# Two blocks on one core: the seventh bunch of experts kept out of four buffers, one weight layout for all bunches, and the normed x written spread

## The reference, cut to what matters

```python
x = layer_norm(DEEPNORM_ALPHA * x + y, ln1_g[layer], ln1_b[layer])
y = hierarchical_moe(x, ...)            # two experts of 32 a token
...
def block_ffn(args):                    # weights 1024x256, 1024x256, 256x1024 each
    xb, e = args
    return (jax.nn.silu(xb @ w_gate[e]) * (xb @ w_up[e])) @ w_down[e]
```

## Time and profile before

| what | value |
|---|---|
| median of three runs | 734.92 us |
| the profiled execution | 740.1 us |
| its span | 738.2 us |
| TensorE (PE) busy | 660.7 us, 89% |
| VectorE (DVE) busy | 352.3 us, 48% |
| ScalarE (ACT) busy | 330.4 us, 45% |
| moved by DMA | 167.84 MB, mean 227 GB/s |

### The profile page before, as it was taken

One profiled execution on the slowest core, in us unless ns is written; L12 is line 12 of the kernel. 1 busy time (PEld: TensorE's weight loads), 2 busy tenths in 40 slices (PEclk: granted clock), 3 DMA queues, 4 the chain that ended last, 5 costly groups with the idle time before them and its releaser, 6 DMA issues.

```text
span 738.2 us, 11783 instructions
## 1 busy us (share of the span) xinstructions
PE 660.7 (89%) x4605; PEld 512.8 (69%) x4606; DVE 352.3 (48%) x817; ACT 330.4 (45%) x776; POOL 43.8 (6%) x57
## 2 busy tenths in 40 slices
PE   6989999999899999969856999998979999889986
PEld 5867998689545644616421589877859899778876
DVE  1543657646511021101000357887774577886643
ACT  3465655531111121202010253777865556888642
POOL 6001000000000000000000132010000020100000
PEclk9999999999999999989885999999989999999999
DMA  9995325896999999999769938026263080081301
GB/s 273 340 287 184 124 65 173 270 304 249 378 387 417 408 415 412 412 417 408 308 209 417 342 103 291 9 72 214 82 204 115 1 265 22 11 275 58 115 1 58
DMA packets 94681, 167.84 MB, mean 227 GB/s; under 512 B 4270, under 2 KB 75712, under 8 KB 90528
## 3 DMA queue, kind: packets, MB, share of 16 engines
q1 hardware_dynamic: 92272, 160.88, 61.1%
q0 software_dynamic: 2224, 6.10, 2.5%
q10 hardware_dynamic: 128, 0.08, 0.0%
HBM read 165.96 MB, written 1.07 MB: 226 GB/s over the span
## 4 chain that ended last, share of the span: by engine, by line
PE 60%; SPq 12%; DVE 9%; DMA 8%; ACT 8%; issue 3%; DVEq 0%; ACTq 0%
PE psum L922 10%; SPq L786 10%; PE psum L923 10%; PE psum L924 10%; PE psum L1337 5%; PE psum L1293 4%; PE psum L1352 2%; PE psum L1227 2%; DMA values<-in_w_expert_up_dram 2%; DMA mixT<-in_w_expert_up_dram 2%; PE psum L965 2%; PE psum L1057 2%; DMA ring<-in_w_in_dram 2%; PE psum L1274 2%; DVE w_low L2349 2%
## 5 line engine op out<-in xcount | busy, mean ns | idle before, releaser
L922 PE MATMUL psum<-a_high,w_high 128*128 128x256 f32 x512 | 150.8, 295 | 9.1 <-DVE w_low L2349 4.6
L923 PE MATMUL psum<-x_low,w_high 128*128 128x256 f32 x512 | 146.0, 285 | 0.0
L924 PE MATMUL psum<-a_high,w_low 128*128 128x256 f32 x512 | 145.9, 285 | 0.0
L922 PEld LDWEIGHTS psum<-a_high,w_high 128*128 128x128 f32 x512 | 99.2, 194 | 18.9 <-issue 6.8
L2349 DVE TENSOR_TENSOR w_low<-ring,w_high 128x1024 fp32r<-128x1024 f32 (+1 forms) x73 | 100.9, 1394 | 17.9 <-ACT w_high L1677 17.9
L1677 ACT ACTIVATE w_high<-ring 128x1024 fp32r<-128x1024 f32 (+1 forms) x79 | 96.1, 1220 | 13.6 <-DMA ring<-in_w_in_dram 10.3
L923 PEld LDWEIGHTS psum<-x_low,w_high 128*128 128x128 f32 x512 | 99.4, 194 | 0.1
L924 PEld LDWEIGHTS psum<-a_high,w_low 128*128 128x128 f32 x512 | 99.3, 194 | 0.0
L1337 PE MATMUL psum<-ring,q_c 128*32 128x512 f32 x336 | 64.9, 708 | 27.0 <-DMA ring<-in_w_expert_up_dram 18.3
L922 PE MATMUL psum<-w_high,a_high 128*128 128x256 f32 x240 | 69.4, 289 | 0.7 <-DVE mix_low L2360 0.7
L1337 PEld LDWEIGHTS psum<-ring,q_c 128*32 128x32 f32 x336 | 16.6, 127 | 64.6 <-issue 63.9
(11 more groups left out here) (346 smaller groups left out, 1175.6 us busy)
## 6 DMA issues: line engine op xcount, KB each, us to landing
ring<-in_w_in_dram SPq DMA_DIRECT2D x36, 1024.0 KB, 9.0
ring<-in_w_expert_down_dram SPq DMA_DIRECT2D x22, 1024.0 KB, 17.3
ring<-in_w_expert_gate_dram SPq DMA_DIRECT2D x42, 512.0 KB, 12.6
ring<-in_w_expert_up_dram SPq DMA_DIRECT2D x42, 512.0 KB, 14.3
ring<-in_w_out_dram SPq DMA_DIRECT2D x12, 1024.0 KB, 5.1
ring<-in_w_mem_kv_dram SPq DMA_DIRECT2D x4, 1024.0 KB, 15.0
k_c<-in_w_expert_down_dram SPq DMA_DIRECT2D x3, 1024.0 KB, 17.4
xT<-in_w_expert_gate_dram SPq DMA_DIRECT2D x4, 512.0 KB, 11.0
```

Source lines behind the costliest of these rows:

```text
L922: pe.matmul(dst, left[0], right[0], start=first, stop=False)
L923: pe.matmul(dst, left[0], right[1], start=False, stop=False)
L924: return pe.matmul(dst, left[1], right[0], start=False, stop=last)
```

## The change

Four things change. `expert_slots` keeps bunch 6 (the seventh) out of the buffers 0 to 3; bunch 7 still takes them for its first four pieces. The gate and up weights of all bunches come in the layout of eight rows a partition. The first norm's centred values go to a part of `tiles` (`centred2`) instead of staying in `x_nat`, and `scaled_half` writes the normed x to `x_nat` spread: channel 8q + k to place 128k + q (`spread` is the view written, `folded_in` the ones read). For tt = 0 two such halves take the place of one whole row. All gathers then read 128 contiguous elements, and the diagonal products of bunch 0 read x through `spread`, so that the sum comes out in natural order. The second norm writes x in natural order as before.

```diff
--- before.py
+++ after.py
@@ -138,7 +138,6 @@
 MORE_SLOTS = (9, 10, 11)
 EXPERT_RING = len(FIRST_LOADS)
 PER_BUNCH = 12
-IN_ORDER = 2
 
 
 def expert_slots():
@@ -146,10 +145,16 @@
     at = [k for _, k in sorted(FIRST_LOADS)]
     free = [k for k in at if k not in ONCE]
     for i in range(len(at), PER_BUNCH * BUNCHES):
-        last = i >= PER_BUNCH * (BUNCHES - 1)
-        j = i % PER_BUNCH
-        at.append(next(k for k in free if not last or (k == NEXT_LAYERS[j] if j < AT_ONCE
-                                                       else k not in NEXT_LAYERS + MORE_SLOTS)))
+        b, j = divmod(i, PER_BUNCH)
+        if b < BUNCHES - 2:
+            k = free[0]
+        elif b == BUNCHES - 2:
+            k = next(k for k in free if k not in NEXT_LAYERS)
+        elif j < AT_ONCE:
+            k = NEXT_LAYERS[j]
+        else:
+            k = next(k for k in free if k not in NEXT_LAYERS + MORE_SLOTS)
+        at.append(k)
         free.remove(at[-1])
         free.append(at[-1])
     return at
@@ -473,6 +478,14 @@
         def bank(n):
             return psum[:, n, :]
 
+        def spread(row, half):
+
+            return row.rearrange("p (k q) -> p q k", k=KC)[:, P // 2 * half:P // 2 * half + P // 2, :]
+
+        def folded_in(row, half):
+
+            return row[:, 512 * half:512 * half + 512].rearrange("p (q k) -> p q k", k=KC)
+
         def c_(name):
             a, b = CONST[name]
             return const[:, a:b]
@@ -481,6 +494,7 @@
         slots = ring[:, :].rearrange("p (s k n) -> p s k n", s=RING, k=KC)
         x2 = x_nat[:, :].rearrange("p (t d) -> p t d", t=2)
         x4 = x_nat[:, :].rearrange("p (t k q) -> p t k q", t=2, k=KC)
+        centred2 = tiles[:, 0:2048].rearrange("p (t d) -> p t d", t=2)
         xT3 = xT[:, :].rearrange("p (k t) -> p k t", k=KC)
         x1T = q_c[:, :].rearrange("p (k t) -> p k t", k=KC)
         y_nat = tiles[:, 0:2048].rearrange("p (t d) -> p t d", t=2)
@@ -782,7 +796,7 @@
                 if j < GATE_UP:
                     half = j // AT_ONCE
                     for m, name in enumerate(("w_expert_gate", "w_expert_up")):
-                        w = ins[name][0, e].rearrange("(k p) n -> p k n" if b < IN_ORDER else "(p k) n -> p k n", p=P)
+                        w = ins[name][0, e].rearrange("(p k) n -> p k n", p=P)
                         sp.dma_start(to[:, SLOT // 2 * m:SLOT // 2 * m + SLOT // 2].rearrange("p (k n) -> p k n", n=DE),
                                      w[:, 4 * half:4 * half + 4, :]).then_inc(loaded[slot_of(n)], 16)
                 else:
@@ -1289,8 +1303,7 @@
                 for c in range(4):
                     k = 4 * half + c
                     for tt in range(2):
-                        x = x4[:, tt] if b < IN_ORDER else x2[:, tt, :].rearrange("p (q k) -> p k q", k=KC)
-                        mm = pe.matmul(dst[:, P * c:P * c + P], x[:, k, :], places2[:, tt, :],
+                        mm = pe.matmul(dst[:, P * c:P * c + P], x4[:, tt, k, :], places2[:, tt, :],
                                        start=(tt == 0), stop=(tt == 1))
                 mm.then_inc(gathered_ready, 1)
 
@@ -1424,7 +1437,7 @@
                     if b == 0:
                         for m in range(4):
                             pe.matmul(bank(m), diagonal[:, P * (m // 2):P * (m // 2) + P],
-                                      x2[:, m // 2, 512 * (m % 2):512 * (m % 2) + 512],
+                                      spread(x2[:, m // 2, :], m % 2),
                                       start=True, stop=False, skip_group_check=True)
                     if b + 1 < BUNCHES:
                         if b > MEM_AT:
@@ -2120,7 +2133,8 @@
                 dve.wait_ge(ready, 32)
                 dve.wait_ge(ln_var, 2 * n + tt + 1)
                 for half in range(2):
-                    op = dve.scalar_tensor_tensor(x_half(tt, half), values(tt, half), mv3[:, tt, 0:1],
+                    to = x_half(tt, half) if n else centred2[:, tt, 512 * half:512 * half + 512]
+                    op = dve.scalar_tensor_tensor(to, values(tt, half), mv3[:, tt, 0:1],
                                                   ln_row[:, 0, 512 * half:512 * half + 512], ALU.subtract, ALU.mult)
                 link(op)
 
@@ -2133,9 +2147,9 @@
 
             def scaled_half(tt, half):
 
-                xs = x_half(tt, half)
-                return dve.scalar_tensor_tensor(xs, xs, ln_rs[:, tt:tt + 1],
-                                                ln_row[:, 1, 512 * half:512 * half + 512], ALU.mult, ALU.add)
+                return dve.scalar_tensor_tensor(spread(x2[:, tt, :], half), folded_in(centred2[:, tt, :], half),
+                                                ln_rs[:, tt:tt + 1], folded_in(ln_row[:, 1, :], half),
+                                                ALU.mult, ALU.add)
 
             def logit_shift(tt):
 
@@ -2468,8 +2482,10 @@
                         tt = job[1]
                         dve.wait_ge(p_ready, j + 1)
                         centred(0, tt, ln1_in, x_half)
+                        dve.wait_ge(ln_rstd, tt + 1)
                         if tt == 0:
-                            scaled(0, 0)
+                            scaled_half(0, 0)
+                            scaled_half(0, 1).then_inc(ln_done, 1)
                         logit_shift(tt)
                         if tt == 1:
                             scaled_half(1, 0)
```

## The result

The changed kernel takes 729.62 us (median of 6 runs) against 736.37 us for the kernel before in 6 runs beside it: a ratio of 0.9899, 95% interval 0.9851 to 0.9946, which is 7.4 us less (the medians are 6.8 apart). One of its six runs took 904.85 us; it lies outside everything else and is not in the ratio. Two more series of the same changed kernel gave 0.9875 and 0.9905. So the kernel became faster, by about half of what was forecast (13.9 us), and 729.62 lies above the range of 716 to 728.5. The profiled execution has a span of 731.0 us, against 738.2 before.

What follows compares the result with a forecast made beforehand. The prediction took the expert stage as bound by transfers, with one self-made stop. Its terms, -13.9 + 1.0 - 1.0 = -13.9 us, led from the median of 734.92 to 721.0 us, range 716 to 728.5.

Steps and rivals of the forecast that it cites:

- What bounds the kernel: Expert stage: bound by transfers at about 413 GB/s, whose stream stops just once, behind bunch 6, for the kernel's own reasons.
- Part 1: Buffers of bunches 6 and 7: the hole in transfers goes, bunch 7's sigmoid at 393.24 instead of 407.18, -13.94 us.
- What is late next: the down weights ... so they aren't: Bunch 7's down weights, all landed at 394.6, would be in time for down products starting at 398.0.
- Part 2: Contiguous x in the gathers of bunches 2 to 7: 4.3 us less each, worth nothing because transfers hide it.
- Part 3: Spread writes of normed x and stepped diagonal products before and in bunch 0: 0 to 3.6 us, taken as +1.0.
- second term: Bunch 0's diagonal products reading x stepped: +4.3 us at 2.2 times, 3.7 covered by transfers, leaving 0 to 0.6.
- rival B: Spread access costs its upper bound: 723.6 us, or 724.6 without the 4 KB runs' microsecond; chance 0.10.
- A: Contiguous gathers slow the transfers by contention, 1.1 us each, six of them 6.6: 727.6 us; chance 0.14.
- C: The stream stops anyway, through SP's flag reading or another wait: some 731 us, at most no change; chance 0.06.
- Part 4: 4 KB runs in bunches 0 and 1 speed their gate and up pieces: -2.1 to 0 us, taken as -1.0.
- D: More idle time keeps the granted clock at its lower level through bunches 4 to 7: 749.5 us; chance 0.04.

Runs made afterwards that it cites:

- the buffers alone: The kernel before with the new choice of buffers and nothing else: ratio 0.9851, median 727.07 us; its repeat 0.9850, median 724.85 us.
- The held loads: The changed kernel with the first five loads of the second block held until bunch 7's down products begin to finish: ratio 0.9846.
- the first repeat: The changed kernel run once more with nothing altered: ratio 0.9875 to the kernel before, median 729.74 us against 738.02.
- The late diagonal products: The changed kernel with bunch 0's diagonal products behind its down products instead of ahead of its gather: ratio 0.9842, median 728.70 us.

## Why the prediction was half right

**What bounds the kernel** was right: transfers, with one stop of the kernel's own making. In the changed kernel TensorE is busy for 43.57 of 60 us between 300 and 360, where it was 48.55, and the stage's period did not move.

**Part 1, the hole, was right in size.** Forecast -13.94 us; the buffers alone gave bunch 7's sigmoid at 393.10 (forecast 393.24) and 13.5 and 12.2 us at the products behind the experts, 11.0 and 12.5 in the timed medians (727.07 against 738.02, 724.85 against 737.34). Some of that closeness is luck: I had TensorE start bunch 7's first half at 376.6, and it started at 384.37, 4.9 us after its last products of bunch 6. I read this as its own flag reading and branching, the only thing that the program has there; two packets of the instruction queues (379.97 and 381.79 in the changed kernel) fall into the same 4.9 us. I had counted this for SP alone. In return the second half, running right behind the first, took 3.64 us and not 6.34: the 2.7 us that I had left to the low end of the range came. In the buffers alone the weights for the second half landed at 387.64 and it began at 389.40, so there it was TensorE, and not the transfer of the forecast, that set the sigmoid's start.

**"What is late next: the down weights ... so they aren't" failed.** This is the first failed step. I put their landing at 394.6, the moment by which the stream's bytes would have moved, with nothing for the lag of a landing behind it. The held loads show how many bytes that is, since their queue is empty behind them: 127.6 MB from the span's start. The buffers alone have moved as much at 395.8 and land at 398.27, a lag of 2.4 us (2.8 in the repeat); the changed kernel at 399.5, 397.2 and 399.2, and it lands at 403.14, 400.98 and 402.36, lags of 3.7, 3.8 and 3.2. I had 3.4 us between landing and use. With the stream nearly on time it almost fits (waits of 0.53 and 1.20 us). In the changed kernel the stream is 2.6 to 4.9 us behind the forecast, and it is a wait of 3.1 us in all three profiles and, in two of them, a lower clock behind it (4.98 and 5.37 us instead of 3.67). The experiment with the held loads shows that at most 0.7 us of it is owed to the loads behind.

**Part 2** was right: the gathers of bunches 2 to 7 take 3.8 us instead of 7.8, and the period from bunch 5 to 6 is 30.46 us where it was 30.57, so they gain nothing.

**Part 3 was mis-sized in its second term, the diagonal products.** This is the second failed step. The spread writes were nearer the low end, as I had chosen: 1.11 against 0.75 us, and the way from the second row's residual to the start of gather 0 grew from 11.30 to 11.82 us, 0.5 us. For the diagonal products I had +4.3 us, covered by 1.5 MB of transfers still under way, so 0 to 0.6. They cost +3.45 us (7.08 against 3.63), and together with the 0.5 us of the writes the restart came 4.0 us later in the first repeat (218.18 against 214.21; 2.0 more in the first profile, which started later as a whole). The cover was even longer than I had read it: the last of the eight pieces landed 7.4 us behind the restart in the kernel before, since the queue still held others ahead of them, and 2.8 us behind it in the changed one. So the queue did not run empty, and by my reckoning next to nothing should have been lost. What failed is that reckoning, that a late issue costs only what the engines stand idle: after the restart they are busy, the rates of 2 us stretches are 324, 348, 301 and 229 GB/s, and 1.0 MB is lost. That is 2.4 us where I had at most 0.6.

The Trainium skill (SBUF — State Buffer, the paragraph on cachelines) charges accesses that fall into a new 16-byte line each time. The runs agree in sign: spread writes took 1.5 times as long on VectorE and the stepped read by TensorE's moving side 1.95 times. That rule was my rival B, the nearest in mechanism. Its 723.6 to 724.6 is still too low, because most of its price came through the transfers behind the late issue and not through the engines' time. A's 727.6 and C's 731 lie nearer by their numbers alone; neither happened.

**Part 4** gave 0.7 us of its 1.0 by 196 us, and it was gone again by 200 us: as the prediction said itself, much of it only becomes idleness before the next issue. The term should have been nothing.

**The other rivals.** A, contention of the gathers, is refuted: during the gather at 366.6 to 370.4 the transfers ran at 404 GB/s, and at 335 to 341 at 407. The 286 of the earlier trace rows was something else: in the changed kernel the same dip comes at 208 to 212 us (328 and 299 GB/s), before that gather, which runs from 211.75 to 215.5 at 409. C, a stream that stops anyway, did not happen; nor did D, as the clock from 300 to 360 is 0.89, after 0.90.

**The range.** Its low end was given as 721.0 - 2.7 - 1.1, which is 717.2 and not 716.

**Open:** why one engine finishes some microseconds behind the others; why packets take long behind a late issue; the 0.6 us not assigned in the sum; and how the 2 to 5 us between the changed kernel and the buffers alone divide between the dip, the gap at 196 to 200 us and the later landing, which follows from them. The late diagonal products (0.9842) and the buffers alone (0.9851) can't be told apart by time.

## What to carry to other kernels

Taking away the one stall of a transfer-bound stage pays in full only if every other feed of the queue stays on time. Look for the issues that come when the queue has little left (here 3.4 us and less), and count for them more than the time the engines would stand idle. Faster transfers shorten the cover of everything that was hidden under them: here 0.3 MB gained by 196 us were lost again by 200. And put a load's landing some microseconds (here 2.4 to 3.8) behind the point at which its bytes have moved, when you ask whether a consumer that is to start earlier will find it.

## What the runs showed of the chip

A queue that is fed again only 2 to 3 us before its end comes back slowly: in the three profiles of the changed kernel it moved 301, 314 and 281 GB/s from 220 to 228 us, at a DMA share of 0.96 to 1.00, where the kernel before moves 401 and 416 in its two profiles. With nothing queued behind it, the last transfer of a long stream landed while the rate had been at 29 GB/s for 2 us: 15 of its 16 arrival marks were there 1.6 us before the last. A stepped moving operand of TensorE takes 1040 ns instead of 592 for 128x512 f32, and a spread result of VectorE 1.11 us instead of 0.75 for 128x512 f32. Between bunches 6 and 7, where the program reads a flag and branches, TensorE is idle for 4.8 to 4.9 us with nothing that it waits for ("<-issue"), in all profiles of the new choice of buffers; before, the hole hid it. And the kernel before ranges from 732.75 to 742.83 us within 17 runs on one chip, the mean granted clock being 0.981 in the one and 0.963 in the other, so differences of 3 us were read from profiles stage by stage as well as from medians.
